# Which experts load their weights four slabs at a time: 2 to 29 in place of 4 to 27

## What is computed

```python
up = xb @ w_up[e] + b_up[e]
glu, lin = up[:, :D_FF_EXPERT], up[:, D_FF_EXPERT:]
glu = jnp.minimum(glu, SWIGLU_LIMIT)
lin = jnp.clip(lin, -SWIGLU_LIMIT, SWIGLU_LIMIT)
act = glu * jax.nn.sigmoid(SWIGLU_ALPHA * glu) * (lin + 1)
return act @ w_down[e] + b_down[e]
```

## Time and profile before

| | us |
|---|---|
| median of 3 runs | 1141.87 (1141.70 to 1141.93) |
| the profiled execution, its own time | 1140.42 |
| its span in the trace | 1138.7 |
| PE busy in the span | 1115.0 |

### The profile page before, as it was taken

One profiled execution on the slowest core, in us unless ns is written; L12 is line 12 of the kernel. 1 busy time (PEld: TensorE's weight loads), 2 busy tenths in 40 slices (PEclk: granted clock), 3 DMA queues, 4 the chain that ended last, 5 costly groups with the idle time before them and its releaser, 6 DMA issues.

```text
span 1138.7 us, 15628 instructions
## 1 busy us (share of the span) xinstructions
PE 1115.0 (98%) x5248; PEld 483.5 (42%) x5249; DVE 362.1 (32%) x909; ACT 215.7 (19%) x401; POOL 84.7 (7%) x206
## 2 busy tenths in 40 slices
PE   8999999999999999999999999999999999999998
PEld 6786487543333333333333333333333333333344
DVE  5899413232322222222222332222222222222223
ACT  5312212121111112111111111111111111111113
POOL 1991000000000000000000000000000000000000
PEclk9999999999999999999999999999999999999999
DMA  9566336489999999999999999999999999999996
GB/s 363 195 259 268 147 148 257 186 363 431 430 435 425 437 428 433 433 432 432 429 436 426 439 427 436 429 432 432 430 435 426 439 427 437 428 425 427 425 424 262
DMA packets 29115, 437.62 MB, mean 384 GB/s; under 512 B 4064, under 2 KB 4704, under 8 KB 12320
## 3 DMA queue, kind: packets, MB, share of 16 engines
q1 hardware_dynamic: 28224, 436.10, 90.4%
q10 hardware_dynamic: 864, 1.14, 0.3%
HBM read 436.18 MB, written 1.05 MB: 384 GB/s over the span
## 4 chain that ended last, share of the span: by engine, by line
PE 84%; DMA 14%; SPq 0%; another core or an unknown queue 0%; issue 0%; DVE 0%; ACT 0%; ACTq 0%; DVEq 0%
PE bank L1841 35%; PE bank L1870 16%; DMA ring<-in_w_up_dram 13%; PE total L1802 5%; PE bank L1789 4%; PE bank L1465 2%; PE bank L1484 2%; PE bank L1878 2%; PE bank L1698 2%; PE bank L1475 2%; PE bank L1796 1%; PE bank L1631 1%; PE total L1631 1%; DMA ring<-in_w_in_dram 1%; PE bank L1996 1%; PE bank L1590 1%
## 5 line engine op out<-in xcount | busy, mean ns | idle before, releaser
L1841 PE MATMUL bank<-ring,buf_m 128*64 128x512 f32 (+1 forms) x2160 | 464.5, 587 | 12.6 <-DMA ring<-in_w_up_dram 12.6
L1841 PEld LDWEIGHTS bank<-ring,buf_m 128*64 128x64 f32 x2160 | 158.2, 138 | 313.1 <-issue 307.0
L1870 PE MATMUL bank<-ring,buf_f 128*64 128x512 f32 x1024 | 232.2, 595 | 0.0
L1353 DVE COPY buf_f<-bank 128x512 f32<-128x512 f32 x32 | 22.1, 692 | 445.7 <-PE bank L1841 445.7
L1870 PEld LDWEIGHTS bank<-ring,buf_f 128*64 128x64 f32 x1024 | 67.9, 136 | 136.1 <-issue 115.0
L884 ACT ACTIVATE buf_f<-buf_f 128x256 f32<-128x256 f32 x32 | 13.3, 416 | 331.7 <-DVE buf_f L1363 331.7
L1802 PE MATMUL total<-buf_m,wr_sb 64*128 64x512 f32 x264 | 65.6, 615 | 0.7 <-ACT buf_m L891 0.7
L1789 PE MATMUL bank<-buf_k,buf_m 128*64 128x512 f32 x264 | 63.9, 605 | 0.0
L650 POOL TENSOR_TENSOR buf_m<-table,buf_m 128x4 f32<-128x4 f32 x33 | 6.6, 199 | 762.7 <-DVE channel_vecs L1340 762.0
L1359 DVE TENSOR_TENSOR buf_f<-bank,buf_m 128x512 f32<-128x512 f32 x64 | 44.0, 687 | 57.8 <-PE bank L1878 57.8
L891 ACT ACTIVATE buf_m<-bank 128x512 f32<-128x512 f32 x32 | 19.1, 598 | 185.3 <-PE bank L1870 185.3
(11 more groups left out here) (386 smaller groups left out, 844.3 us busy)
## 6 DMA issues: line engine op xcount, KB each, us to landing
ring<-in_w_up_dram SPq DMA_DIRECT2D x48, 4096.0 KB, 33.2
ring<-in_w_down_dram SPq DMA_DIRECT2D x24, 4096.0 KB, 31.7
ring<-in_w_up_dram SPq DMA_DIRECT2D x29, 2048.0 KB, 15.8
ring<-in_w_down_dram SPq DMA_DIRECT2D x12, 2048.0 KB, 13.6
ring<-in_w_down_dram SPq DMA_DIRECT2D x7, 1024.0 KB, 36.4
ring<-in_w_up_dram SPq DMA_DIRECT2D x6, 1024.0 KB, 36.9
ring<-in_w_in_dram SPq DMA_DIRECT2D x4, 1024.0 KB, 17.1
ring<-in_w_xkv_dram SPq DMA_DIRECT2D x2, 2048.0 KB, 27.2
```

Of the source, the lines that this page charges most:

```text
L1841: ins = t_.matmul(banks[bank][h * 64:(h + 1) * 64, c0:c1], xg[:, k, :], w[:, :, k % 4, h, :], start=first, stop=last)
L1870: ins = t_.matmul(banks[2][h * 64:(h + 1) * 64, :], actT[:, f, :], group(p, UPS + f // 4)[:, lo + h * BANK:lo + (h + 1) * BANK], start=f = ...
```

## The change

Two numbers of one constant: experts 2, 3, 28 and 29 move from the narrow form to the wide form and into the loops. All bytes, matmuls and steps stay as they are.

```diff
-WIDE_FROM, WIDE_TO = 4, 28
+WIDE_FROM, WIDE_TO = 2, 30
```

## The result

| | before | changed |
|---|---|---|
| median of 12 runs, us | 1141.9 (1140.41 to 1143.52) | 1143.34 (1142.34 to 1146.05) |
| ratio | | 1.0018, 95% interval 1.0011 to 1.0026 |
| span of the profiled run | 1138.7 | 1140.6 |

The changed kernel is 2.1 us slower by the ratio (0.0018 x 1141.9): clear of zero, and just inside the 0.2% that the prediction took as the least change worth calling one. The profiled span is 1.9 us longer, as forecast.

A forecast was written before the change was run, and what follows sets the result against it. TensorE waiting for up-weight transfers bounds it, the end hanging on expert 30's third group at 1082.41. Hole, savings and four-slab wait move that to 1084.3: 1141.87 + 1.9 = 1143.8 us, likeliest 1143.2 to 1144.9, 8 in 10 1141.4 to 1145.9.

The forecast's parts named there:

- rival A: Clock falls after expert 29's stop, the last one: 1.7 us more, 3.6 us slower in all, 1145.5 us; chance 0.33.
- Part 1: At expert 2's first 4 MB transfer, issued at 247.61, the transfer queue runs dry once: a hole of 2.1 us (1.7 to 2.6).
- does not run dry a second time: At expert 2's down transfer, issued at 267.11: no second hole taken, or one of 0.6 us.
- Rival B: At expert 2 the queue doesn't run dry; the end moves by -0.2 to -0.4 us, 1141.5 us; chance 0.1.
- Part 2: Fewer, larger transfers give back 0.5 us for experts 2 and 3, and 0.5 us for experts 28 and 29.
- Part 3: Near the end, fewer TensorE program blocks fetched through queue 8: 0.4 us back at expert 29's landing, bounds 0 and 0.5.
- expert 30's stop: Before its third up group TensorE stopped 2.19 us, ending at 1082.41; forecast to vanish, covering part of its 4.3 us delay.
- 5.4 us gap: Between landings at 1051.5 and 1056.9, where 4.9 is usual; read as a program packet's delay, 0.4 us counted back.
- Part 4: Expert 29's second half waits for four slabs: stop of 2.6 us to 1057.7, leaving expert 30's third group 1.9 us later.
- low clock: After stops of about 2.55 us, a half of 16 instructions takes 8.78 us instead of 7.09; at most every second expert.

The follow-up runs named there:

- e3_hole: Kernel before, with only the first 2 MB transfer of expert 2 waiting for expert 0's second up step instead of its first: ratio 1.0020, +2.01 us.
- e5_split30: Changed kernel with expert 2's first four up slabs as two 2 MB transfers, issued at up steps 1 and 2: ratio 1.0022, +2.14 us against before.
- e1_front: Kernel before with experts 2 and 3 also wide (2 to 27), the early half of the change alone: ratio 1.0007, +0.73 us.
- e2_tail: Kernel before with experts 28 and 29 also wide (4 to 29), the late half of the change alone: ratio 0.9997, 0.00 us.
- e10: Changed kernel with expert 2's first four up slabs and its four down slabs as two 2 MB transfers each: ratio 1.0023, +2.58 us against before.
- e6_split28: Experts 2 to 27 wide, as e1_front, with expert 2's first four up slabs as two 2 MB transfers: ratio 1.0011, +1.63 us against before.
- e9_split2_28: Experts 2 to 27 wide, as e1_front, with expert 2's first four up slabs and four down slabs as two 2 MB transfers each: ratio 0.9994, -0.77 us.
- e12_gfinal: e9_split2_28 with the final gain's transfer issued ahead of the last two pieces of expert 31: ratio 0.9994, -0.75 us against before.
- e4_pairwait: Kernel before, transfers unchanged, with TensorE at expert 29 waiting for both groups of a pair before starting the first: ratio 1.0006, +0.37 us.
- e7: Changed kernel profiled again without an edit: 852.86 us from expert 0 to expert 30's combine, +3.89 us against before.
- e8: Changed kernel profiled a further time without an edit: 851.37 us from expert 0 to expert 30's combine, +2.40 us against before.

## Why the prediction was right, point by point

**The sum.** Forecast: span 1140.6, and 1.9 us over the median. Measured: 1140.6, and 2.1 us by the ratio. The two medians are only 1.4 us apart (1143.34 - 1141.9); both kernels scatter by 3 us or more, and the ratio uses all their runs. That the span agrees to a tenth is in part luck: from expert 0 on the changed kernel is 2.20 us later, and its stages before expert 0 happened to be 0.27 shorter (240.21 against 240.48). The median is in part luck too, as it lies between two groups of runs (see rival A).

**Part 1, the hole.** Right in kind, and e3_hole shows it alone at +2.01 us against 2.1 assumed. In the profile the delay was 1.9 us at the first landing and 1.85 at expert 27's stop (997.82 to 999.67); counted from expert 0, 2.2 and 2.1. The term after the gain of part 2 was put at 1.6, so 0.25 to 0.5 us too small. The Trainium skill ("DMA: Bandwidth & Descriptors", Anatomy of one DMA) has a fixed cost of about 2 us for one transfer, fitted to transfers that GpSimd issues. The ones here come from the sync engine. Into an empty queue they agree: in e3_hole the 2 MB issued at 247.41 land after 7.2 us, 2.3 more than the 4.9 of a flowing stream. In a full queue they don't. The claim that the queue does not run dry a second time held in the changed kernel, by the cover of the first hole. Rival B rested on the reverse, that taking the first hole away would free the stream, and e5_split30 shows that it would not.

**Part 2, fewer transfers.** The landings vary by as much, but the bytes tell. DMA of the kernel before and then of e1_front, from 0 to 840 us after the start of expert 0:

```profile
DMA packets 26287, 417.60 MB, mean 386 GB/s; under 512 B 3742, under 2 KB 4382, under 8 KB 11358
```

```profile
DMA packets 25335, 416.81 MB, mean 385 GB/s; under 512 B 3634, under 2 KB 4274, under 8 KB 11250
```

By 840 us after the start of expert 0 the kernel before had moved 417.60 MB and e2_tail 417.82; the changed kernel had moved 417.02 and e1_front, whose end is narrow, 416.81. At 432 GB/s both differences are 0.5 us for experts 28 and 29, as forecast. For experts 2 and 3 no gain is seen: by 80 us after expert 0 both the changed kernel and e3_hole had moved 89.20 MB, where 0.5 us would be 0.2 MB.

**Part 3, program blocks.** The packets fell from 19 to 15 (17 in either half), 0.25 MB / 15 = 16.7 KB each. The Trainium skill ("Runtime: NRT & Kernel Launch", Instruction fetch mechanics) has blocks of 16 KiB, and calls their cost mostly hidden; here no wait of TensorE for its program was looked for, only what the packets do to the data. The trace keeps the time of each of the 16 increments of a landing. In the kernel before they lie 1.8 us apart at 1051.5, 2.3 at 1056.9 and 3.3 at 1082.3, the landing that ends expert 30's stop. Packets on queue 8 came in the microseconds from 1050 and from 1080, just ahead of the two rises. The same is seen early: e10's rise at 289.9 (above), and in the kernel before 0.8 us at 248.4 and 1.6 at 258.9, with a packet from 254, which makes those two landings 10.6 us in place of 9.8. So the mechanism of the prediction is there, but a packet counts only where it makes the last engine later: in e1_front those of 1058 and 1087 leave the 2.1 us as they are. Two numbers then give an estimate of the end of each kernel whose last experts are narrow, and it is within 0.15 us of what was measured: the delay of the stream, by the bytes moved up to 840 us after expert 0 (417.60 MB before, at 432 GB/s), and the distance between the first and the last increment at the landing that ends expert 30's stop:

| kernel | MB by then | stream later by, us | distance, us | less 3.3 | sum | measured |
|---|---|---|---|---|---|---|
| e1_front | 416.81 | 1.8 | 2.1 | -1.2 | +0.6 | +0.73 |
| e3_hole | 416.81 | 1.8 | 3.4 | +0.1 | +1.9 | +2.01 |
| e6_split28 | 416.87 | 1.7 | 3.3 | 0.0 | +1.7 | +1.63 |
| e9_split2_28 | 417.50 | 0.2 | 2.4 | -0.9 | -0.7 | -0.77 |
| e12_gfinal | 417.50 | 0.2 | 2.4 | -0.9 | -0.7 | -0.75 |

e6_split28 has as few packets as e1_front (17) and the distance of before: the number of blocks doesn't set it. In the changed kernel the distance is 2.1 us at expert 29's second half, against 2.3 at the landing of 1056.9 before, so of the 0.4 us that I took no more than 0.2 is seen there. The 5.4 us gap before 1056.9 was a poor row to build on, as e4_pairwait, with the same packets, has 4.9 there.

**Part 4, four slabs at expert 29.** The landing was put at 1057.6, the start at 1057.7 and expert 30 at 1077.3; measured 1057.97 and 1077.53, and the stop of expert 30 is gone. Counted from expert 0 the second half starts 1.33 us later than the fourth group did before, where 0.8 was forecast (1057.7 - 1056.91); the stream's delay and the return from the blocks were both taken 0.2 us or more too kindly. One row came out otherwise: a stop of 2.6 us was forecast and 0.87 is in the profile, since this time the low clock fell on expert 28. As the stop ends with the landing, the end is the same. The forecast's own pattern, a full stop of 2.65 us with the half behind it at 7.09, came only in e5_split30.

**The two parts together.** By the traces +0.73 and 0.00 add to less than the +2.20 of both. The early half delays the stream by 1.8 us, but the end of that kernel hangs on expert 30's third landing, whose increments happened to lie 1.2 us closer together than before; without that it would be near the +2.01 of e3_hole. The late half moves the end from that landing to expert 29's second half and uses up the stop that covered it, at no cost by itself (e2_tail). With both, the whole delay of the stream arrives at the one landing from which TensorE runs to the end without a stop.

**Rival A** is no rival but a second outcome of the same kernel: e7 has it in full (852.86, 1.7 over the first profile), e8 does not. Six of the 12 runs lie at 1143.7 to 1146.1, six at 1142.3 to 1143.0. The mean granted clock of the run is 0.991 to 0.993 in the first six and 0.994 or 0.995 in the others, which points to the clock; since the stages ahead of expert 0 vary by as much, how many are due to a low clock at expert 29 stays open.

## What to carry to other kernels

A larger transfer that waits for the last of its regions is issued later than the first small one was; whether that costs anything is read from the queue's depth at that moment, and the landing of the transfer ahead is a late sign of it: here the engines stood still before it, so 1.5 us of notice was none. Where a stream of transfers sets the pace, a hole in it near the start goes through to the end. And a larger transfer next to the end should be asked which stop covers it: the late half cost nothing alone, but it left no stop behind it, neither for a late stream nor for a low clock.

## What the runs showed of the hardware

- Into an empty queue a transfer lands 2.3 us (2 MB, e3_hole) to 3.6 us (4 MB, the changed kernel: 13.3 in place of 9.7, with 1.1 of it from one engine behind the others) late. The engines are idle before the last landing shows it: no data moved from 247 to 248 us, and that landing was at 247.7. An issue 1.5 us before the landing ahead left a hole (e5_split30, 33 GB/s), issues 4.2 us before (2 MB, the kernel before) and 4.4 us before (4 MB, e10_split2_30) left none; the bound between is open.
- The low clock came behind most stops of 2.45 us or more, with 8.5 to 8.8 us for the half. In the 14 traces, from 880 us on, it was 38 of 46 such stops; one of the others is the half of 7.09 us at 910.39. Behind a low clock the next stop was shorter and had none, so that at most every second expert has one, and which of them differs between executions of one kernel.
- The 16 increments of one landing lie 1.8 to 3.4 us apart in the last 60 us of the stream, and TensorE's wait ends with the last. A block of the program is a packet on queue 8 of about 1 us (two of them are 0.2% of 16 engines over 65 us). It raised that distance by 0.5 and 1.0 us near the end of the kernel before, by 1.3 in e10_split2_30, and not at all near the end of e1_front. That the packet is the cause is read from its place just ahead of each rise; no run moves a packet alone.
